# Plain fp32 matmuls on the weights as they landed, in place of three products of rounded halves

## The reference

```python
# first model: two layers, modulated by mod = silu(c) @ w_mod[i] + b_mod[i]
y = einsum('bsgi,gio->bsgo', pooled, w_pool)      # layer 0, four groups of 256
x = x + g2 * (relu(h @ w_up[i]) ** 2 @ w_down[i]) # both layers, 1024 -> 4096 -> 1024
q, k, v = split(h @ w_qkv, 3)                     # layer 1, 1024 -> 3072
y = attention(q, k, v) @ w_o                      # 16 heads, causal
x1 = rmsnorm(x, norm_final)
# second model: 16 meta tokens ahead of x1 (272 rows), one layer
p = rmsnorm(h) @ w_in_2                           # 1024 -> 3600, to two mixers
x2 = x1 + concat(gated_delta_rule(...), forgetting_attention(...)) @ w_out_2
out = rmsnorm(x2 + (silu(h @ w_gate_2) * (h @ w_up_2)) @ w_down_2)  # 2816 wide
```

## Time and profile before

| | |
|---|---|
| device time, median of 3 runs | 1230.55 us (1228.34 to 1230.89) |
| the profiled execution, first to last instruction | 1229.1 us |
| TensorE busy | 1098.8 us, 5513 matmul records |
| VectorE busy | 681.5 us, 1074 instructions, of it 314.0 us at L1049 |
| ScalarE busy | 451.5 us, 748 instructions, of it 267.9 us at L557 |
| GpSimd busy | 109.6 us |
| mean granted TensorE clock | 0.892 of full |
| HBM read | 193.76 MB, mean 159 GB/s |

### The profile page before, as it was taken

One profiled execution on the slowest core, in us unless ns is written; L12 is line 12 of the kernel. 1 busy time (PEld: TensorE's weight loads), 2 busy tenths in 40 slices (PEclk: granted clock), 3 DMA queues, 4 the chain that ended last, 5 costly groups with the idle time before them and its releaser, 6 DMA issues.

```text
span 1229.1 us, 14350 instructions
## 1 busy us (share of the span) xinstructions
PE 1098.8 (89%) x5513; PEld 927.8 (75%) x5513; DVE 681.5 (55%) x1074; ACT 451.5 (37%) x748; POOL 109.6 (9%) x108
## 2 busy tenths in 40 slices
PE   5489999999799898899999879999869689999995
PEld 5488777777698688678888669986659677777774
DVE  5487666776645894544444366623373545554453
ACT  1113433433444321444444345542222334443342
POOL 2000100101000000010010010001074000000000
PEclk9976999999799657899999869985679988999998
DMA  9876577677354653154454513540000023545510
GB/s 342 286 271 228 211 253 266 208 270 271 140 206 151 206 192 138 71 200 160 185 196 177 188 47 131 203 137 1 1 1 1 19 85 103 183 159 191 185 68 34
DMA packets 105178, 195.47 MB, mean 159 GB/s; under 512 B 2283, under 2 KB 46572, under 8 KB 105132
## 3 DMA queue, kind: packets, MB, share of 16 engines
q1 hardware_dynamic: 104380, 192.58, 44.6%
q0 software_dynamic: 752, 2.26, 0.5%
HBM read 193.76 MB, written 1.07 MB: 159 GB/s over the span
## 4 chain that ended last, share of the span: by engine, by line
PE 70%; DVE 16%; ACT 5%; issue 5%; DMA 3%; POOL 1%; SPq 1%; DVEq 0%; ACTq 0%; POOLq 0%
PE ps L1593 16%; PE ps L1632 12%; PE ps L1661 10%; PE ps L1858 6%; DVE wl L1049 5%; PE ps L1749 4%; DMA raw<-in_w_mod 3%; PE ps L2077 3%; DVE arena L909 2%; PE ps L1543 2%; ACT wh L557 2%; DVE arena L936 2%; PE ps L1993 1%; ACT arena L574 1%; PE ps L1762 1%
## 5 line engine op out<-in xcount | busy, mean ns | idle before, releaser
L1049 DVE TENSOR_TENSOR wl<-raw,wh 128x1024 fp32r<-128x1024 f32 (+1 forms) x288 | 314.0, 1135 | 306.1 <-ACT wh L557 305.8
L557 ACT ACTIVATE wh<-raw 128x1024 fp32r<-128x1024 f32 (+1 forms) x288 | 267.9, 982 | 364.6 <-PE ps L1593 135.1
L1593 PE MATMUL ps<-wh,H 128*128 128x512 f32 x288 | 117.5, 408 | 6.1 <-DVE L L1032 3.3
L1593 PE MATMUL ps<-wl,H 128*128 128x512 f32 x288 | 116.2, 403 | 0.0
L1593 PE MATMUL ps<-wh,L 128*128 128x512 f32 x288 | 115.4, 401 | 0.0
L1661 PE MATMUL ps<-wh,aTh 128*128 128x512 f32 x256 | 103.2, 403 | 8.9 <-DVE wl L1049 8.9
L1632 PE MATMUL ps<-wh,H 128*128 128x512 f32 x256 | 103.4, 404 | 2.4 <-DVE wl L1049 2.4
L1661 PE MATMUL ps<-wl,aTh 128*128 128x512 f32 x256 | 102.7, 401 | 0.0
L1661 PE MATMUL ps<-wh,aTl 128*128 128x512 f32 x256 | 102.5, 400 | 0.0
L1632 PE MATMUL ps<-wl,H 128*128 128x512 f32 x256 | 101.4, 396 | 0.0
L1632 PE MATMUL ps<-wh,L 128*128 128x512 f32 x256 | 101.2, 395 | 0.0
(11 more groups left out here) (373 smaller groups left out, 1943.2 us busy)
## 6 DMA issues: line engine op xcount, KB each, us to landing
raw<-in_w_up SPq DMA_DIRECT2D x16, 2048.0 KB, 7.5
raw<-in_w_down SPq DMA_DIRECT2D x16, 2048.0 KB, 7.7
raw<-in_w_mod SPq DMA_DIRECT2D x12, 2048.0 KB, 9.7
raw<-in_w_in SPq DMA_DIRECT2D x7, 2048.0 KB, 7.5
raw<-in_w_mod SPq DMA_DIRECT2D x12, 1024.0 KB, 7.5
raw<-in_w_qkv SPq DMA_DIRECT2D x6, 2048.0 KB, 10.9
raw<-in_w_mod SPq DMA_DIRECT2D x8, 1536.0 KB, 7.0
raw<-in_w_gate SPq DMA_DIRECT2D x11, 1024.0 KB, 5.3
```

Source lines behind the costliest of these rows:

```text
L557: e.activation(dst, src, ACT.Copy).then_inc(S["split_h"], 1)
L1049: e.tensor_tensor(o, src, i1.bitcast(F32), ALU.subtract).then_inc(S["split_l"], 1)
L1593: ins = e.matmul(ps[:, bank, :], src[xa][:, 4 * hb + k, META + P * m:META + P * m + P], w[wb][:, k, :], start=(hb == 0 and k == 0 and n == 0),
```

## The change

`split` on both engines, `split_h`, both aT subtractions, the pool's rounding, `wh`, `wl`, `H`, `L`, `aTh`, `aTl` and the semaphores `split_h`, `split_l`, `hs_h`, `hs_l`, `tl_done`, `gtl_done` go. TensorE multiplies `hf` (or `aT`, the hidden rows as ScalarE copies them) with the slot of `raw` directly, one plain f32 matmul for each pair of blocks, and waits for the load itself. A slot is loaded again when TensorE has used its tile (`w_used`). The memory of the removed tiles stays reserved. `w_o`'s first tile is loaded after the modulation units of the attention stage instead of before them (N_WO is 55 in place of 47), since it can no longer wait in wh and wl. The core of the diff (the other product loops change in the same way):

```diff
-            def free_split(t):
-                e.wait_ge(S["split_l"], 4 * t + 4)
+            def tile_used(t):
+                e.wait_ge(S["w_used"], 2 * t + 2)
...
                 if u == 7:
-                    free_split(T_POOL)
+                    tile_used(T_POOL)
                 load_mod0(u)
...
             e.wait_ge(S["mod_accu"], 5)
+            load(N_WO % R, kview(N_WO % R), wo[:, :, 0:512])
+            e.wait_ge(S["mod_accu"], 6)
             load(N_WO1 % R, kview(N_WO1 % R), wo[:, :, 512:1024])
 
-            e.wait_ge(S["mod_accu"], 6)
+            e.wait_ge(S["mod_accu"], 7)
             load(1, kview(1), wup[1][:, :, 0:512])
...
                 if fresh[0] is not None and k % 2 == 0:
-                    e.wait_ge(S["hs_l"], fresh[0] + k // 2 + 1)
+                    e.wait_ge(S["hf_done"], 8 * fresh[0] + k + 2)
...
-            def up(it, t, mods_in=None):
-
+            def up(it, slot, land, mods_in=None):
+
+                e.wait_ge(raw_in[slot], land)
+                w = kview(slot)
                 for hb in range(2):
-                    half(t, hb)
-                    w = [q[:, hb, :].rearrange("p (k n) -> p k n", k=4) for q in (wh, wl)]
                     for m in range(NM):
...
-                        for k in range(4):
-                            parts(4 * hb + k)
-                            for n, (xa, wb) in enumerate(PASSES):
-                                ins = e.matmul(ps[:, 4 + m, :], (H, L)[xa][:, 4 * hb + k, META + P * m:META + P * m + P],
-                                               w[wb][:, k, :], start=(hb == 0 and k == 0 and n == 0),
-                                               stop=(hb == 1 and k == 3 and n == 2))
+                        for k in range(4 * hb, 4 * hb + 4):
+                            parts(k)
+                            ins = e.matmul(ps[:, 4 + m, :], hf[:, k, META + P * m:META + P * m + P], w[:, k, :],
+                                           start=(k == 0), stop=(k == KD - 1))
                         if hb == 1 and m == 0:
                             ins.then_inc(S["u_done"], 1)
-                    ins.then_inc(S["split_used"], 1)
+                    ins.then_inc(S["w_used"], 1)
...
-            def down(it, t, last=False):
-
-                e.wait_ge(S["tl_done"], 2 * it + 2)
+            def down(it, slot, land, last=False):
+
+                e.wait_ge(S["th_done"], 2 * it + 2)
+                e.wait_ge(raw_in[slot], land)
+                w = dview(slot)
```

More of the change, by code:

```diff
@@ L242, in before, with g_slot @@
             return 16 * len([i for i in range(N_FFN) if i % R == n % R])
+        def g_slot(n, i=0):
+            seen = sum(2 if (k - N_FFN == 0 or (k - N_FFN) % 2 == 1) and k != N_FFN + 21 else 1
+                       for k in range(N_FFN, n + 1) if k % R == n % R)
+            step = 32 if (n - N_FFN) % 2 == 1 else 16
+            return n % R, before(n) + 16 * seen + step * i
         def kview(s):
@@ L325, in _ @@
             load(1, kview(1), wqkv[:, :, 0:512])
[L326 to L329, removed]
+            for i in range(1, 6):
+                tile_used(T_QKV + i - 4)
+                load((N_QKV + i) % R, kview((N_QKV + i) % R), wqkv[:, :, 512 * i:512 * i + 512])
             for u in range(NMU):
                 if u < R:
-                    free_split(T_QKV + 3 + u)
+                    tile_used(T_QKV + 2 + u)
                 else:
@@ L537, in _ @@
             e.activation(ftab[:, :], ps[0:HEADS, 6, 0:NDIST], ACT.Copy, scale=float(DH) ** 0.5).then_inc(S["f_sb"], 1)
[L539 to L557, removed]
             nnorm = [0]
@@ L1144, in _ @@
             mod_cols(8)
-            split(T_MLP0, landed(N_MLP0)[0])
             mod_cols(9)
@@ L1728, in _ @@
             gate_mm(4)
-            down(7, T_MLP0 + 15, last=True)
+            down(7, *landed(40), last=True)
             e.wait_ge(S["gate_set"], 4)
@@ L2068, in g_turn, with g_down @@
                 ins.then_inc(S["gt_done"], 1)
-            def g_down(j, t, last=False):
-                e.wait_ge(S["gtl_done"], j + 1)
-                for hb in range(2):
-                    half(t, hb)
+            def g_down(j, slot, land, last=False):
+                e.wait_ge(S["gth_done"], j + 1)
+                e.wait_ge(raw_in[slot], land)
+                w = raw[:, slot, 0:HALF].rearrange("p (k n) -> p k n", k=2)
+                for k in range(2):
                     for m in range(NM):
                         for c in range(2):
-                            for n, (xa, wb) in enumerate(PASSES):
-                                ins = e.matmul(ps[:, 2 * m + c, :], (aTh, aTl)[xa][:, hb, P * m:P * m + P],
-                                               (wh, wl)[wb][:, hb, 512 * c:512 * c + 512], start=False,
-                                               stop=(last and hb == 1 and n == 2))
-                            if last and hb == 1 and 2 * m + c < 3:
+                            ins = e.matmul(ps[:, 2 * m + c, :], aT[:, k, P * m:P * m + P], w[:, k, 512 * c:512 * c + 512],
+                                           start=False, stop=(last and k == 1))
+                            if last and k == 1 and 2 * m + c < 3:
                                 ins.then_inc(S["y_done"], 1)
-                    ins.then_inc(S["split_used"], 1)
-            g_up(0, T_FFN)
+                    ins.then_inc(S["w_used"], 1)
+            g_up(0, N_FFN % R, before(N_FFN) + 32)
             g_turn(0)
```

377 lines of the change are left out of this document (102 added, 275 removed).

## The result

The changed kernel takes 1365.87 us (median of 4 runs, 1360.93 to 1366.59) where the kernel before takes 1230.72 us (4 runs, 1228.34 to 1231.21): a ratio of 1.1109, 95% interval 1.1073 to 1.1146. The forecast was 1392 us with a range from 1368; the direction is right and the size is off by 2%, but the time is 2 us under the low end, and both large terms of the sum were off, one up, one down. The profiled run of the changed kernel took 1366.59 us, its span is 1364.9 us, 135.8 us more than before.

What follows compares the result with a forecast made beforehand. The prediction took TensorE to bound the kernel: 1229.1 us of span, +184 for dearer f32 products, -23 for waits given back, make 1390, and 1.5 more for the median gives 1392 us; range 1368 to 1458.

Steps and rivals of the forecast that it cites:

- Rivals 1 to 4: Product loops: per-column rate 1458 us (0.13); f32 record at fp32r cost about 960 (0.02); chain's split 1329 (0.03); half clock 1469 (0.04).
- the 86 us of the chain: The split's 5% and 2% of the chain, claimed to go entirely, giving 1329 us; chance 0.03.
- I take 8 ns over for each record: TensorE's product loops: each f32 record runs 8 ns over its stream, 0.870 us a pair at 512 columns.
- +184: TensorE's product loops: total added price of the plain f32 matmuls in us, between +164 and +247.
- the idle time ahead of the seven product groups is 22.4 us: TensorE's waits behind wl or L: 22.4 us idle, adjusted by -3, +2 and +2 to 23 us given back.
- -26: Waits ahead of the product groups: the most time in us expected back; -19 the least, -23 taken.
- What moves: Slots come free later, after the multiplication; later loads in MLP0, the start-up and attention were expected to cost nothing.
- MLP0's slots and w_o at nothing: MLP0 loads have 13.9 us to land against 7.7; w_o tiles load late in attention but in time: no cost.
- The start-up at 0: `w_mod` loads waiting for the pool products at the start: 0 to 3 us late, taken as 0.
- rival 5: Late loads: MLP0's down tile by 3 us in seven rounds, the start by 3 to 6; 1417 us, chance 0.06.
- the pure stream: Product loops, low price: f32 records cost only their streamed columns, 0.853 us a pair at 512 columns, +164 us.

Runs made afterwards that it cites:

- E5: The kernel before, with the second and third record of each pair in `up` cut to 64 of 128 stationary columns: 1213.53 us, ratio 0.9857.
- E3: The kernel before with its split halves, token parts and transposed parts rounded to bf16, still three products: 1184.84 us, ratio 0.9645.
- E4: The changed kernel with the pool weights landing in memory of their own, so modulation loads don't wait for the pool products: 1362.55 us, ratio 1.1089.
- E8: The changed kernel itself, measured again: 1364.02 us, ratio 1.1109.
- E9: The changed kernel with the pool weights in memory of their own, run beside the repeated changed kernel: 1361.01 us, ratio 1.109.
- E1: The changed kernel's products with all split work back and TensorE's old waits for it; first w_o tile split behind attention: 1402.44 us, ratio 1.1412.
- E7: The kernel before with four products a tile, the third done twice, all split work and waits kept: 1452.19 us, ratio 1.1799.
- E2: The changed kernel's products with all split work back, but TensorE waiting for none of it: 1361.93 us, ratio 1.1048.
- E6: The kernel before with two of its three products a tile, all split work and waits kept: 1051.98 us, ratio 0.8549.
- E10: The kernel before with bf16 halves in four buffers instead of two each: 1164.31 us, ratio 0.9467.

## Why the prediction was right or wrong

**Bound, direction, counts.** Right. TensorE bounds both kernels, an f32 matmul is two records that stream twice each, 888, 192 and 144 pairs, and the clock is 1.00 in the loops. Rivals 1 to 4 are out: a pair costs 0.858 and not 0.928 or 0.464, the 86 us of the chain did not go, and no product loop lost the clock.

**The failing step on the price: "I take 8 ns over for each record".** It is 2.5 ns: 0.429 instead of 0.435 a record, +169 us instead of +184. I placed the f32 record between L1870's 3 ns and fp32r's 19 ns because the new shape has a full weight load beneath its stream. E5 shows that the weight load was never the reason (1.5 ns for 54 ns less of it), and E3 that the 19 ns belong to the type. The row of the same instruction, L1870, was the one to take as it stood. The Trainium skill's estimate quoted in the prediction (page "TensorE: Matmul & The Clock Gate", Back-to-back issue gap), 0.858 us a pair, is what the trace has. The same section warns that its formula gives too much at 512 columns in a stream of loads and matmuls, 216 ns against 131 measured; the bf16 records of E3, in such a stream, start 0.2158 us apart, which disagrees with the 131 and fits the formula.

**The failing step on the give-back: "the idle time ahead of the seven product groups is 22.4 us" as a measure, and -26 as a bound.** 33 us came back. Some 11 of them are in rounds: 0.9 us in six of MLP0 and 0.55 in ten of the FFN, of which the groups of before show 0.3 a round or nothing. Idle time is counted from a record's modelled end, and a record of 0.40 us with the next start 0.232 later hides every wait below 0.17 us and that much of each longer one. That is some 6 us in the rounds. Period less count times distance is the measure that doesn't hide: 24.91 - 96 x 0.2325 = 2.6 against a floor of 1.7, and both ends were in the trace of before (MLP1's rounds have 0.87 outside, and the eight modulation matmuls take 0.89). The granted clock is the other missing part. At 0.50 the product loops lost 21 us of clock in the trace of before and 16 in that of the changed kernel, where I had counted 2 us for it: the first 11.20 us of w_o stood at 0.85 before and the first 13.70 at 1.00 after, those of w_out at 0.73 and 0.89. In E4, E8 and E9 the product loops lost 13 to 19 us, so this part is 2 to 8 us, 5 in the pair of traces compared here.

**The reason given for the give-back was wrong too.** I put it down to the split that goes. In the loops it is the longer product that covers the split: E1 keeps the split and the waits and has the changed kernel's rounds; E7 has the same parts outside its products with fp32r. What the removal itself brings stands where stages begin and end. Some 22 of the 33 us lie there, clock included, and how they divide between the removal, the longer product and the clock was not separated; E1 against E2 (37 us between the two spans) bounds the removal only from above, since 7.3 us of it are the w_o tile that I moved and 6.8 the late slot. A cheaper product, which the kernel's engineer might want next, would have met the split and not TensorE (E6: -178 us where the products fell by 247).

**What moves: MLP0's slots and w_o at nothing.** Right: no DMA releases a product, and QKV and attention together stayed 2.7 us under their price. **The start-up at 0** was wrong by 2.7 us net, of which 1.2 are the pool's price, and by about 7 gross in the traces (E9); rival 5 (1417 us) was far too large.

1392 - 15 for the price - 10 for what came back = 1367, against 1365.87 measured. The range ended at 1368 because its low end took the pure stream and -26 and then was not widened below; I treated the counted idle time as a bound, which it is not.

## To carry to other kernels

- Judge a wait in a loop by the round's period less the products at their measured distance, and look for the same floor in another loop; the idle time of a pipelined TensorE is a lower bound only.
- Work on VectorE and ScalarE that sits beside TensorE is not a stock of time to be won back: ask which product would be long enough to cover it. Where it isn't covered, a second set of buffers can do it (E10: rounds at the floor, 20 us below E3 by the medians).
- Three products of a cheap type beat one f32 matmul on this engine (0.696 or 0.648 against 0.858 us a pair): count streams, not instructions.

## What the runs showed of the hardware

- **The type sets the distance of records, not the weight load.** At 512 columns fp32r takes 0.2317 to 0.2333 us, bf16 0.216, and f32 0.429 for two streams. An f32 record of 272 columns takes 0.229, two streams of 0.113 and 2.5 ns, with a 190 ns weight load beside it, as long as fp32r's 188. What in the type sets the excess was not tested by itself. bf16's weight load is 98 ns (E3).
- **VectorE held up by GpSimd.** In the four traces without split work (the changed kernel, E4, E8, E9) one `Kb` multiplication of 128x512 takes 6.76 us, in the eight with it (before, E1 to E3, E5 to E7, E10) 1.53. The changed kernel, then E2, in order of time:

```profile
993.75 6.76 DVE L1228 TENSOR_TENSOR Kb<-k_t,coef 128x512 f32<-128x512 f32 x1
993.95 2.03 POOL L501 TENSOR_TENSOR arena<-v_t,beta 128x512 f32<-128x512 f32 x2
995.94 1.03 POOL L502 TENSOR_TENSOR R1m<-kv_m,beta 16x512 f32<-16x512 f32 x1
...
1000.44 1.52 DVE L1228 TENSOR_TENSOR Qn<-q_t,nrm 128x512 f32<-128x512 f32 x1
```

```profile
993.15 1.53 DVE L1409 TENSOR_TENSOR Kb<-k_t,coef 128x512 f32<-128x512 f32 x1
994.60 1.52 DVE L1409 TENSOR_TENSOR Qn<-q_t,nrm 128x512 f32<-128x512 f32 x1
995.53 1.48 POOL L509 TENSOR_TENSOR R1m<-kv_m,beta 16x512 f32<-16x512 f32 x1
```

In E2 the two engines take turns here, 1.5 us each; in the changed kernel GpSimd runs six of its instructions at about 1.0 us before VectorE gets its turn. It also goes the other way: from 999.87 in E2 one GpSimd instruction takes 3.88 us beside four of VectorE's at 0.67. The stage is as long in both (268.6 and 268.7 us). The Trainium skill, page "SBUF — State Buffer", Who interferes with whom, says that a VectorE instruction with two inputs in SBUF contends with a GpSimd instruction that reads it; the rows agree. What decides between taking turns and waiting for several was not tried.
